# First two tiles of the first layer computed in turn, block by block, with the second weight slab loaded and split early

## The reference

```
h = rms_norm(x, g_mix);  z = h @ w_in            # 1024 -> 10752 columns, shared by all mixers
ya = retention(qa, ka, va) ; yb = spatial_gating(ub, vb) ; yc = dilated attention, 3 groups of 4 heads
merged = sum over b of sigmoid(gate_b) * (y_b @ w_branch[b])
x = x + merged @ w_o
h = rms_norm(x, g_ffn);  x = x + (silu(h @ W_gate) * (h @ W_up)) @ w_down
rms_norm(x, g) = x * rsqrt(mean(x*x) + 1e-6) * g
```

## Time and profile before

| | us |
|---|---|
| median of 3 runs | 1954.92 (1954.76 to 1955.07) |
| the profiled execution | 1955.0 |
| its span in the trace | 1953.2 |
| PE busy | 1934.8, 99% of the span |
| DVE busy | 1135.9, 58% |
| ACT busy | 776.7, 40% |

### The profile page before, as it was taken

The page is one execution under the profiler, slowest core; times in us unless marked ns, Lnnn a source line. Parts: engine busy times, 40 slices in busy tenths (PEclk is TensorE's granted clock), DMA queues, the critical chain, the costliest instruction groups (busy, mean ns, idle before and its releaser), DMA issues. The chain is left out here.

```text
span 1953.2 us, 23528 instructions
## 1 busy us (share of the span) xinstructions
PE 1934.8 (99%) x9368; PEld 1690.0 (87%) x9368; DVE 1135.9 (58%) x1523; ACT 776.7 (40%) x1090; POOL 0.2 (0%) x4
## 2 busy tenths in 40 slices
PE   7999999999999999999999999999999999999999
PEld 6888888888888888888888888888888888888888
DVE  6666667746666554355476666676366664534545
ACT  5544444533334432233345444344343343322334
POOL 0000000000000000000000000000000000000000
PEclk9999999999999999999999999999999999999999
DMA  5222222233233233333232222222223332333333
GB/s 193 87 77 76 87 82 81 92 98 98 96 120 107 97 99 98 106 107 99 97 98 92 66 79 84 82 88 94 100 97 107 109 108 97 97 97 108 98 103 123
DMA packets 65436, 191.67 MB, mean 98 GB/s; under 512 B 17200, under 2 KB 17456, under 8 KB 65328
## 3 DMA queue, kind: packets, MB, share of 16 engines
q1 hardware_dynamic: 65328, 190.17, 30.2%
HBM read 187.98 MB, written 2.16 MB: 97 GB/s over the span
## 5 line engine op out<-in xcount | busy, mean ns | idle before, releaser
L663 PE MATMUL bank<-h_high,w_high 128*128 128x512 f32 x2048 | 787.9, 385 | 12.3 <-DVE h_low L999 10.7
L663 PE MATMUL bank<-h_high,w_low 128*128 128x512 f32 x2048 | 777.0, 379 | 0.0
L663 PE MATMUL bank<-h_low,w_high 128*128 128x512 f32 x2048 | 776.9, 379 | 0.0
L829 ACT ACTIVATE w_high<-raw 128x1024 fp32r<-128x1024 f32 x342 | 360.9, 1056 | 951.8 <-PE bank L663 941.1
L994 DVE TENSOR_TENSOR w_low<-raw,w_high 128x1024 fp32r<-128x1024 f32 x342 | 417.1, 1222 | 91.3 <-ACT w_high L829 77.7
L663 PEld LDWEIGHTS bank<-h_high,w_high 128*128 128x128 f32 x2048 | 387.8, 189 | 70.4 <-issue 8.3
L663 PEld LDWEIGHTS bank<-h_high,w_low 128*128 128x128 f32 x2048 | 387.5, 189 | 55.1
L663 PEld LDWEIGHTS bank<-h_low,w_high 128*128 128x128 f32 x2048 | 387.9, 189 | 53.6
L663 PE MATMUL bank<-in_high,w_high 128*128 128x512 f32 x672 | 254.9, 379 | 0.0
L663 PE MATMUL bank<-in_low,w_high 128*128 128x512 f32 x672 | 254.7, 379 | 0.0
L663 PE MATMUL bank<-in_high,w_low 128*128 128x512 f32 x672 | 254.7, 379 | 0.0
(11 more groups left out here) (106 smaller groups left out, 1070.4 us busy)
## 6 DMA issues: line engine op xcount, KB each, us to landing
raw<-weights SPq DMA_DIRECT2D x343, 512.0 KB, 3.5
row<-rows SPq DMA_DIRECT2D x3, 768.0 KB, 4.5
xT<-x_t SPq DMA_DIRECT2D x8, 256.0 KB, 5.7
decay_sb<-decay SPq DMA_DIRECT2D x8, 256.0 KB, 3.8
out_t<-xT SPq DMA_DIRECT2D x8, 256.0 KB, 6.5
sgw<-spatial SPq DMA_DIRECT2D x3, 256.0 KB, 2.6
rot<-rotation SPq DMA_DIRECT2D x1, 512.0 KB, 7.8
pairs_by_token<-pairs SPq DMA_DIRECT2D x16, 4.0 KB, 4.9
```

What stands on the lines that cost most here:

```text
L663: return pe.matmul(o, w, m, start=start, stop=stop)
L829: act.activation(w_high[:, PART_SLOT[s], :, :], raw[:, s % RAW_SLOTS, :, :], ACT.Copy).then_inc(part_high_w.sem, 1)
```

## The change

Three edits.

1. `SECOND_SLAB_AT` goes from 4 to 0: SP issues the DMA of slab 1 right behind x block 0.
2. In the prologue ACT and DVE split slab 1 after block `SECOND_SLAB_AT` instead of after the block behind it, hence after block 0 instead of after block 5.
3. PE walks a list of its own in the first layer: tile 0 block 0, tile 1 block 0, tile 0 block 1, tile 1 block 1 and so on to block 7, and then STEPS without the main products of tiles 0 and 1. The second layer, and the lists of all other engines, stay.

```
-SECOND_SLAB_AT = 4
+SECOND_SLAB_AT = 0
...
+def in_turn_at_the_start():
+
+    first = [("main", i, k, k + 1) for k in range(KT) for i in range(2)]
+    return first + [s for s in STEPS if not (s[0] == "main" and s[1] < 2)]
+
+
+FIRST_STEPS = in_turn_at_the_start()
...
-                for kind, *key in STEPS:
+                for kind, *key in FIRST_STEPS if base == 0 else STEPS:
...
-                if n == SECOND_SLAB_AT + 1:
+                if n == SECOND_SLAB_AT:
                     split(0, 1)
```

## The result

| | before | after |
|---|---|---|
| median of 22 runs, us | 1955.08 (1954.76 to 1955.60) | 1958.43 (1957.23 to 1959.19) |
| the profiled execution | 1955.0 | 1957.42 |
| its span | 1953.2 | 1955.6 |

The ratio is 1.0017, 95% interval 1.0010 to 1.0023: slower by 3.35 us. The forecast was 1955.4 with a range up to 1957.9. The median lies outside it, and on the side of rival A.

A forecast was written before the change was run, and what follows sets the result against it. Tile 2's start, held by a chain over DVE's prologue and slab 3's DMA, was taken as the bound. Profiled 1955.0, DVE stall +0.5, all else 0, gives 1955.5; less 0.1 for the median, 1955.4, range 1954.6 to 1957.9.

The forecast's parts named there:

- rival A: PE's clock falls while PE waits ahead of tile 2, which starts at 1.2 GHz: +2.0 us, 1957.4; chance 0.24.
- What bounds the kernel: Start of tile 2, 27.09 us, set by a chain: DVE's prologue, a DMA, ACT, DVE, bcast, DVE.
- What was cover becomes idle time: Tile 1 matmuls moved from around stat and bcast: 4.5 us of PE work off the chain, gain 0, idleness hurting only by the clock.
- The stall on DVE: In DVE's prologue, a new wait for w_high of slab 1 behind h_low 0: +0.5 us, bounds 0.2 and 1.2.
- The landing of slab 3: DMA of slab 3 ahead of ACT's split: still 3.8 us from issue to landing, priced 0.
- PE keeps up: In the prologue, PE's stat ends at 22.6 with the clock's rise at 13.9, off the chain: cost 0.
- Rival B: PE doesn't keep up in the prologue at the low clock, the stat holds the chain: up to +5.6 us, 1960.6; chance 0.05.
- Rival C: PE's stat and the matmuls behind it set tile 2's start, so 4.5 us are won: 1950.9; chance 0.04.
- The sign of being wrong: The forecast is wrong if tile 2 starts before 26.5 or after 28.5 us.
- its sign for A: If the clock falls, matmuls start 0.43 us apart after 27.6 us, at the start of tile 2.

The follow-up runs named there:

- experiment 8: The changed kernel with the norm's square root and reciprocal moved ahead of slab 3's split on ACT and DVE: 1953.23 us, ratio 0.9993.
- experiment 9: The kernel before, without the change, with the square root and reciprocal moved ahead of slab 3's split: 1953.94 us, ratio 0.9997.
- experiment 2: The changed kernel with 12 unused matmuls added between stat and bcast and 8 between bcast and tile 2: 1955.79 us, ratio 1.0004.
- experiment 7: The kernel before with only PE's new order, slab 1 still issued behind x block 4: 1962.54 us, median of four runs, ratio 1.0037.
- experiment 4: The changed kernel with only blocks 0 to 2 of tile 1 in turn, its last five blocks left where they stood: 1955.72 us, ratio 1.0005.
- experiment 1: The changed kernel again, same instructions, for a second profile: 1958.27 us, ratio 1.0016 against the kernel before.
- experiment 5: The changed kernel with 12 unused matmuls added between stat and bcast only, nothing behind the bcast: 1955.89 us, ratio 1.0007.

## Why the prediction was wrong, by its steps

*What bounds the kernel: right.* PE lay on the chain with the bcast alone. Moving 4.5 us of its work won nothing, and experiment 8 shows by what the start of tile 2 was held: with the square root ahead of slab 3's split it starts 2.0 us earlier and the median falls by 5.0 us. Experiment 9 agrees in its faster runs (median 1.1 us lower), but its interval takes in no change.

*"What was cover becomes idle time", priced 0: the step that failed.* The likeliest case took the clock to survive the stretch from 22.6 to 27.6. It fell in both profiles, and none of 33 timed runs came under 1957.2. The prediction had the mechanism as rival A, with 0.24; experiment 2 confirms it (filled, 2.5 us come back). Its two grounds for the 0 did not hold. The first was that the bcast cuts the stretch in two: both profiles show the fall ahead of the bcast, and in experiments 7 and 8 it came 0.6 and 0.7 us behind one that had run at full clock. The Trainium skill, TensorE: Matmul & The Clock Gate, Part 4, says that transposes do not count as PE activity in the same way; experiments 7 and 8 agree with it, but no run here tells a bcast that doesn't count from one that is too short. The second was that the clock had stayed high in the thin stretch of the kernel before: experiment 9 has the same prologue, and there it fell. One trace had been taken for what the kernel always does. The exact condition for a fall stays open (experiment 4).

*Rival A's price, 2.0: near, by errors that partly cancel.* It let all of a low stretch of 4.0 us fall into tile 2. Measured, the low stretch lasted 6.8 us in both profiles, but began before the bcast, so only 3.3 and 3.8 us of it lay in tile 2 and cost 1.59 and 1.85. Left out was that the bcast, which is on the chain, runs at the low clock as well (+0.47 and +0.48). Together the clock costs 2.1 to 2.3 us in the two profiles. A's own 1957.4 is still 1.0 below the median. In experiment 1's profile, which is nearer to it, the clock was 0.3 above A's price and the delay of the reciprocal 0.4 above the forecast's 0.5; the latter comes next.

*The stall on DVE, +0.5: right in kind, too small as the whole delay.* The idle time was 0.47 and 0.24 us in the changed kernel. Over all profiles with slab 1 behind x block 0 it runs from 0.22 to 1.19, which are the bounds of the prediction, 0.2 and 1.2; most often it is the lower one. Slab 1 landed at 2.11 + 5.2 = 7.3 instead of 7.5 in the first profile. Missing was the slowing of h_low, 0.32 and 0.64 us in all; with it the reciprocal came 0.38 to 0.93 us late. The prediction took the durations of the rows as fixed. The 0.38 is near the forecast 0.5 by luck, because slab 0 landed 0.27 us sooner in that execution.

*The landing of slab 3: right.* 3.7 us in both profiles, against 3.8 before. The 3.2 us estimated from the Trainium skill, DMA: Bandwidth & Descriptors, "Anatomy of one DMA", did not appear.

*PE keeps up: right in both profiles.* The stat ran from 21.66 to 22.61, forecast 21.7 to 22.6, with the rise of the clock near 14.1, forecast 13.9. How close that is was luck: in experiment 1 the rise came near 11.8 and the stat started at 20.59, in experiment 5 near 16.1 and 23.03. Rival B needed the early slab gone (experiment 7), and a late rise showed only behind a filler (experiment 5). *Rival C* is refuted by experiment 2: with the clock held, nothing is won.

*The sign of being wrong did not catch it.* Tile 2 started at 27.93 and 28.49, inside the 26.5 to 28.5 that the prediction allowed, because more than half of the loss comes behind that start. The spacing of 0.43 us, its sign for A, did.

## What to carry to other kernels

Before moving an engine's work forward, ask what it covered where it stood: PE's matmuls behind the stat kept the clock up. Moving work pays after the chain behind it has been shortened: the change that lost 3.4 us by itself was part of a kernel 3.7 us faster than the one before, once the square root no longer stood behind a weight load and a few blocks were left to fill the waits. One trace in which the clock stays up doesn't show that it always does: look at the spread of the runs as well. In-order queues hide such a chain: look for a small operation queued behind one that waits for a DMA.

## What the runs showed of the hardware

- TensorE's clock rose 3.4 to 8.0 us after the first matmul in profiles of kernels that start alike, by the spacing of the matmuls (0.43 us before, 0.22 after; experiment 1 near 11.8 from 8.43, the change near 14.1 from 8.05, experiment 5 near 16.1 from 8.08). A plan that needs an early rise works in some executions only. Until the first rise the clock column reads 1.00 although matmuls start 0.43 us apart.
- The length of a single pause does not tell whether the clock falls. It stayed over one of 2.74 us (experiment 4). It fell 1.75 us into the pause behind the stat in the change, 3.9 us into it in experiment 1; in experiment 7 after a pause of 1.21 us, the bcast and 0.6 us more; in experiment 9 with no pause above 1.48 us in front of it.
- The runs of some variants spread over 2 to 4 us or fall into two groups (experiments 4, 5, 8, 9), where the kernel before spreads over 0.8 to 1.4. In the profiles of slower executions of experiments 8 and 9 the clock had fallen. In experiment 5's it was a late landing of slab 1 and a late rise with the filler behind it, and experiment 4's slower ones were not profiled.
- DVE's h_low (128x512) took 0.86 to 0.92 us in most rows in which PE ran without pauses at 2.4 GHz, and 0.74 to 0.81 where it paused or ran at 1.2. In the change and in experiments 1 and 5 the longer rows begin right behind the rise of the clock. That the one causes the other was not tested by itself.
